# State-space outputs with tables moving and chunk columns stationary, turned by TensorE instead of through DRAM

## The reference

```python
# u: (B, S, 1024) as 64 groups of 16 channels, 64 complex states per group
bu = complex(einsum('bsgc,gpc->sbgp', ug, real(b_bar)), einsum(..., imag(b_bar)))
_, states = associative_scan(combine, (a_seq, bu), axis=0)
y = einsum('sbgp,gcp->bsgc', real(states), c_re) - einsum('sbgp,gcp->bsgc', imag(states), c_im)
y = y.reshape(B, S, 1024) + d_skip * uf
y = gelu(y)                       # then: (y @ w_glu_v) * sigmoid(y @ w_glu_g)
```

## Time and profile before

| what | value |
|---|---|
| median of 3 runs | 2946.89 us (2944.17 to 2947.73) |
| profiled execution, span of its instructions | 2941.0 us |
| TensorE busy | 2853.5 us (97%) |
| DVE, ACT, POOL busy | 968.6, 753.5, 390.1 us |
| mean granted TensorE clock | 0.988 |

### The profile page before, as it was taken

One profiled execution on the slowest core, in us unless ns is written; L12 is line 12 of the kernel. 1 busy time (PEld: TensorE's weight loads), 2 busy tenths in 40 slices (PEclk: granted clock), 3 DMA queues, 4 the chain that ended last, 5 costly groups with the idle time before them and its releaser, 6 DMA issues.

```text
span 2941.0 us, 34655 instructions
## 1 busy us (share of the span) xinstructions
PE 2853.5 (97%) x13773; PEld 2382.2 (81%) x13773; DVE 968.6 (33%) x1043; ACT 753.5 (26%) x828; POOL 390.1 (13%) x599
## 2 busy tenths in 40 slices
PE   4999999999999999999889999999999999999997
PEld 3888888888788888888678888888888888888886
DVE  4223322231232332242343232333324233333326
ACT  3222321230322222232332222222222222222223
POOL 7729007761000000000000000000000000000000
PEclk9999999998999999999999999999999999999999
DMA  5534643345333333343223323322332333232322
GB/s 133 154 123 131 123 117 94 94 95 127 92 95 97 96 97 95 99 165 99 94 72 96 97 95 97 96 97 93 100 96 96 98 94 99 93 100 93 100 93 100
DMA packets 254302, 303.44 MB, mean 103 GB/s; under 512 B 25344, under 2 KB 214848, under 8 KB 253344
## 3 DMA queue, kind: packets, MB, share of 16 engines
q1 hardware_dynamic: 235112, 265.88, 29.6%
q0 software_dynamic: 7888, 29.83, 4.0%
q10 hardware_dynamic: 11240, 6.85, 0.8%
HBM read 284.23 MB, written 18.28 MB: 103 GB/s over the span
## 4 chain that ended last, share of the span: by engine, by line
PE 95%; DVE 2%; DMA 1%; ACT 1%; issue 0%; POOL 0%; ACTq 0%; DVEq 0%
PE ps L310 21%; PE ps L311 21%; PE ps L312 21%; PE ps L347 7%; PE ps L349 7%; PE ps L348 7%; PE ps L328 2%; PE ps L332 2%; PE ps L330 2%; PE ps L580 1%; PE ps L577 1%; DMA prm<-in_ssm_log_dt 1%; PE ps L539 1%; DVE a_lo L960 1%; PE ps L555 0%; PE ps L506 0%
## 5 line engine op out<-in xcount | busy, mean ns | idle before, releaser
L298 DVE TENSOR_TENSOR w_lo<-raw,w_hi 128x1024 fp32r<-128x1024 f32 x488 | 614.1, 1258 | 1513.3 <-ACT w_hi L294 1513.3
L310 PE MATMUL ps<-a_hi,w_hi 128*128 128x512 f32 x2432 | 954.3, 392 | 3.3 <-DVE w_lo L298 1.2
L311 PE MATMUL ps<-a_lo,w_hi 128*128 128x512 f32 x2432 | 949.7, 391 | 0.0
L312 PE MATMUL ps<-a_hi,w_lo 128*128 128x512 f32 x2432 | 949.7, 391 | 0.0
L294 ACT ACTIVATE w_hi<-raw 128x1024 fp32r<-128x1024 f32 x488 | 516.7, 1059 | 1617.5 <-PE ps L312 1065.7
L310 PEld LDWEIGHTS ps<-a_hi,w_hi 128*128 128x128 f32 x2432 | 458.7, 189 | 102.7 <-DVE w_lo L298 2.8
L312 PEld LDWEIGHTS ps<-a_hi,w_lo 128*128 128x128 f32 x2432 | 458.5, 189 | 96.0
L311 PEld LDWEIGHTS ps<-a_lo,w_hi 128*128 128x128 f32 x2432 | 458.9, 189 | 94.1
L347 PE MATMUL ps<-w_hi,f_hi 128*128 128x512 f32 x704 | 273.9, 389 | 0.0
L348 PE MATMUL ps<-w_lo,f_hi 128*128 128x512 f32 x704 | 273.9, 389 | 0.0
L349 PE MATMUL ps<-w_hi,f_lo 128*128 128x512 f32 x704 | 273.9, 389 | 0.0
(11 more groups left out here) (212 smaller groups left out, 2080.6 us busy)
## 6 DMA issues: line engine op xcount, KB each, us to landing
raw<-in_w_in SPq DMA_DIRECT2D x152, 512.0 KB, 3.6
raw<-in_w_ffn_gate SPq DMA_DIRECT2D x88, 512.0 KB, 3.5
raw<-in_w_ffn_up SPq DMA_DIRECT2D x88, 512.0 KB, 3.5
raw<-in_w_ffn_down SPq DMA_DIRECT2D x88, 512.0 KB, 3.7
raw<-in_w_out SPq DMA_DIRECT2D x32, 512.0 KB, 3.7
raw<-in_w_glu_v SPq DMA_DIRECT2D x16, 512.0 KB, 3.5
raw<-in_w_glu_g SPq DMA_DIRECT2D x16, 512.0 KB, 3.5
h_d<-hc POOLq DMA_DIRECT2D x8, 576.0 KB, 3.4
```

The source lines that it names most:

```text
L298: nc.vector.tensor_tensor(w_lo[:, m % 2, :], raw[:, m % 4, :], w_hi[:, m % 2, :].bitcast(F32), ALU.subtract).then_inc(lo_ready, 1)
L310: nc.tensor.matmul(o, wh[:, k, cols], x_hi[:, kt0 + k, :], start=first and k == 0, stop=False)
L311: nc.tensor.matmul(o, wh[:, k, cols], x_lo[:, kt0 + k, :], start=False, stop=False)
L312: mm = nc.tensor.matmul(o, wl[:, k, cols], x_hi[:, kt0 + k, :], start=False, stop=last and k == 3)
```

## The change

The operands of the output matmuls change places: 64 columns of `u_all` or `s_t` are stationary and the 128 columns of a table move. The result has chunks in partitions (64 per half `gh`) and four groups x 8 positions x 16 channels in columns, so that one octet fills half of the partitions of two PSUM banks. Both halves are issued together behind a piece, `gh` innermost; `pe_chunk_inputs` gets the same order of loops. `s_t` gets a column of zeros in front, so that all 64 columns are used, and the scan takes one step less. DVE copies into `y_tok`, `pe_outputs_turned` turns it with eight transposes per pair of octets, and gelu reads PSUM. The stores to `y_d` and loads of `y_in` are gone; `h_r` has three buffers; the `B_AU` pieces use two pairs of banks instead of four.

```diff
-GELU_AT = ((), (0,), (1, 2), (3,), (4,), (5,), (6, 7), ())
+GELU_AT = ((), (), (0, 1), (2, 3), (4, 5), (6, 7), (), ())
...
-        s_t = at_kb("s_t", 160, [P, HG, 2, NCH])
+        s_t = at_kb("s_t", 160, [P, HG, 2, NCH + 1])
...
-        h_r = [at_kb(f"h_r{s}", kb, [P, OG, 2, P]) for s, kb in enumerate((185, 140, 124, 128))]
+        h_r = [at_kb(f"h_r{s}", kb, [P, OG, 2, P]) for s, kb in enumerate((185, 124, 128))]
+        y_tok = [at_kb(f"y_tok{q}", kb, [P, L, P]) for q, kb in enumerate((140, 177, 181, 120))]
...
-                if k == 5:
-                    sp.wait_ge(y_copied, OCT)
-                    store_outputs(sp, 1)
...
-            for gh in range(2):
-                for e in range(OG):
-                    for ri in range(2):
+            for e in range(OG):
+                for ri in range(2):
+                    for gh in range(2):
...
+            for e in range(OG):
+                for gh in range(2):
+                    g = group(b, gh, e)
+                    nc.tensor.matmul(out(gh, e), u_all[:, g, :], t_q[b // 2][:, g % 16, :], start=e == 0, stop=False,
+                                     skip_group_check=True)
+            for e in range(OG):
                 for ri in range(2):
-                    mm = nc.tensor.matmul(ps[:, bank, col + 1:col + NCH], h_r[b % 4][ph, e, ri, :],
-                                          s_t[ph, OG * b + e, ri, 0:NCH - 1], start=False, stop=True,
-                                          skip_group_check=True)
+                    for gh in range(2):
+                        ph = slice(NST * gh, NST * gh + NST)
+                        mm = nc.tensor.matmul(out(gh, e), s_t[ph, OG * b + e, ri, 0:NCH], h_r[b % 3][ph, e, ri, :],
+                                              start=False, stop=e == OG - 1 and ri == 1, skip_group_check=True)
+            mm.then_inc(y_made, 1)
+
+        def pe_outputs_turned(pe, q):
+
+            pe.wait_ge(y_copied, 2 * q + 2)
+            if q:
+                pe.wait_ge(gelu, 2 * q)
+            for l in range(L):
+                mm = nc.tensor.transpose(pair(3)[:, l * P:l * P + P], y_tok[q][:, l, :], ident[:, :])
+            mm.then_inc(y_turned, 1)
...
-                if k >= 4:
-                    pe.wait_ge(au_copied, k - 3)
-                piece_f(pe, B_AU + k, 0, k % 4, at_hi, at_lo, 0, True, True, lambda: pe_outputs(pe, k + 6, 0))
-                pe_outputs(pe, k + 6, 1)
+                else:
+                    pe.wait_ge(au_copied, k - 1)
+                piece_f(pe, B_AU + k, 0, k % 2, at_hi, at_lo, 0, True, True)
+                if k < 2:
+                    pe_outputs(pe, k + 6)
+                elif k < 6:
+                    pe_outputs_turned(pe, k - 2)
...
-                act.wait_ge(y_back[t % 4], 16 * (t // 4 + 1))
+                act.wait_ge(y_turned, t // 2 + 1)
...
+                if k == 6:
+                    act.wait_ge(y_turned, 4)
```

More of the change, by code:

```diff
@@ L131, in build @@
         at_lo = at_kb("at_lo", 152, [P, HEADS, SEQ], F32R)
-        s_t = at_kb("s_t", 160, [P, HG, 2, NCH])
-        sc = at_kb("sc", 176, [P, 3, 768])
-        p_t = at_kb("p_t", 185, [P, 2, 768])
+        s_t = at_kb("s_t", 160, [P, HG, 2, NCH + 1])
+        sc = at_kb("sc", 176.25, [P, 3, 768])
+        p_t = at_kb("p_t", 185.25, [P, 2, 768])
         a_raw = at_kb("a_raw", 140, [HG, 2, 2 * NST])
@@ L164, in build @@
         y_lo = at_kb("y_lo", 191.75, [P, SSM // P, SEQ], F32R)
-        y_in = at_kb("y_in", 177, [P, 4, SEQ])
         y_act = at_kb("y_act", 185, [P, 2, SEQ])
@@ L184, in build @@
         u_d = nc.dram_tensor("u_d", [L, SSM, NCH], F32, kind="Internal").ap()
-        y_d = nc.dram_tensor("y_d", [L, SSM, NCH], F32, kind="Internal").ap()
         g_d = nc.dram_tensor("g_d", [OCT, P, OG * 2 * P], F32, kind="Internal").ap()
@@ L249, in build @@
         scan_step = sem("scan_step")
-        h_in = [sem(f"h_in{s}") for s in range(4)]
+        s_zero = sem("s_zero")
+        h_in = [sem(f"h_in{s}") for s in range(3)]
         t_in = [sem(f"t_in{q}") for q in range(4)]
@@ L253, in build @@
         y_copied = sem("y_copied")
-        y_stored = [sem(f"y_stored{h}") for h in range(2)]
-        y_back = [sem(f"y_back{s}") for s in range(4)]
+        y_turned = sem("y_turned")
         gelu = sem("gelu")
@@ L363, in build @@
         out_cls = out[0].rearrange("(j c) d -> c j d", c=CLS)
[L365 to L369, removed]
         block = ctx.enter_context(nc.Block())
@@ L559, in pe_chunk_inputs, with y_bank @@
             mm.then_inc(s_made, 1)
[L561 to L573, removed]
-            for e in range(OG):
[L575 to L578, removed]
-                for ri in range(2):
-                    mm = nc.tensor.matmul(ps[:, bank, col + 1:col + NCH], h_r[b % 4][ph, e, ri, :],
-                                          s_t[ph, OG * b + e, ri, 0:NCH - 1], start=False, stop=True,
-                                          skip_group_check=True)
-            if gh == 1:
-                mm.then_inc(y_made, 1)
+        def y_bank(b, gh):
+            return 4 + (b + gh) % 2
@@ new lines, in pe_outputs, with out @@
+        def pe_outputs(pe, b):
+            if b == 0:
+                pe.wait_ge(scan_step, 3 * (NCH - 2))
+                pe.wait_ge(s_zero, 1)
+                pe.wait_ge(heads_lo, 16)
+            pe.wait_ge(h_in[b % 3], 16 * (b // 3 + 1))
+            pe.wait_ge(t_in[b // 2], 16 * L)
+            if b >= 2:
+                pe.wait_ge(y_copied, b - 1)
+            def out(gh, e):
+                return ps[NST * gh:NST * gh + NST, y_bank(b, gh), e * P:e * P + P]
+            for e in range(OG):
+                for gh in range(2):
[3 more added lines that the diff above has]
+            for e in range(OG):
+                for ri in range(2):
+                    for gh in range(2):
[3 more added lines that the diff above has]
+            mm.then_inc(y_made, 1)
@@ L627, in _ @@
             for k in range(8):
-                piece_f(pe, B_G0 + k, 0, k // 4, a_hi, a_lo, 4 * (k % 4), k % 4 == 0, k % 4 == 3,
-                        lambda: pe_outputs(pe, k - 2, 0))
-                pe_outputs(pe, k - 2, 1)
+                piece_f(pe, B_G0 + k, 0, k // 4, a_hi, a_lo, 4 * (k % 4), k % 4 == 0, k % 4 == 3)
+                if k >= 2:
+                    pe_outputs(pe, k - 2)
             for k in range(8):
@@ L633, in _ @@
                     pe.wait_ge(gated, START + k + 1)
-                if k == 2:
-                    pe.wait_ge(y_copied, OCT)
-                if k >= 4:
-                    pe.wait_ge(au_copied, k - 3)
-                piece_f(pe, B_AU + k, 0, k % 4, at_hi, at_lo, 0, True, True, lambda: pe_outputs(pe, k + 6, 0))
-                pe_outputs(pe, k + 6, 1)
+                else:
[5 more added lines that the diff above has]
+                    pe_outputs_turned(pe, k - 2)
             pe.wait_ge(au_copied, 8)
@@ L845, in act_gelu @@
             def act_gelu(t):
-                if t == 0:
-                    act.wait_ge(y_made, OCT)
-                act.wait_ge(y_back[t % 4], 16 * (t // 4 + 1))
+                act.wait_ge(y_turned, t // 2 + 1)
                 if t >= 2:
@@ L852, in act_gelu @@
                 nc.scalar.activation(y_act[:, t % 2, :].rearrange("p (c n b) -> p b c n", b=2, c=CLS),
-                                     y_in[:, t % 4, :].rearrange("p (b c n) -> p b c n", b=2, c=CLS),
+                                     pair(3).rearrange("p (b c h n) -> p h b c n", b=2, c=CLS, h=2)[:, t % 2],
                                      ACT.Gelu_apprx_tanh).then_inc(gelu, 1)
@@ L860, in _ @@
                 act.wait_ge(piece_done, B_AU + k)
-                nc.scalar.activation(mrg[:, 2 * k - 2:2 * k, :].rearrange("p a n -> p (a n)"), pair((k - 1) % 4),
+                if k == 6:
+                    act.wait_ge(y_turned, 4)
+                nc.scalar.activation(mrg[:, 2 * k - 2:2 * k, :].rearrange("p a n -> p (a n)"), pair((k - 1) % 2),
                                      ACT.Copy).then_inc(au_copied, 1)
@@ L1127, in dve_chunk_inputs @@
                 dve.wait_ge(s_made, b + 1)
-                nc.vector.tensor_copy(s_t[:, OG * b:OG * b + OG, :, :].rearrange("p e r n -> p (e r n)"),
-                                      ps[:, 6 + b % 2, :]).then_inc(s_copied, 1)
+                if b == 0:
+                    nc.vector.memset(s_t[:, :, :, 0:1], 0.0).then_inc(s_zero, 1)
+                nc.vector.tensor_copy(s_t[:, OG * b:OG * b + OG, :, 1:NCH + 1].rearrange("p e r n -> p (e r) n"),
+                                      ps[:, 6 + b % 2, :].rearrange("p (a n) -> p a n", n=NCH)).then_inc(s_copied, 1)
             dve_qkv(1, 0, lambda k: dve_chunk_inputs(k - 3) if 3 <= k < 3 + OCT else None)
@@ L1138, in dve_outputs @@
                 for gh in range(2):
-                    g = group(b, gh, 0)
-                    ins = nc.vector.tensor_copy(u_all[:, g:g + OG, :].rearrange("p e n -> p (e n)"),
```

(25 more changed lines are left out.)

## The result

The changed kernel takes 2894.22 us (median of 4 runs, 2892.4 to 2898.64), beside 2947.31 us for the one before on the same chip: a ratio of 0.9828, 95% interval 0.9816 to 0.984, 53 us less. The profiled execution's span is 2892.1 us, beside 2941.0. First the page after the change: span, busy time, clock in 40 slices.

The account below looks back on a forecast made before the run. TensorE, busy 97% of the span, bounds the kernel. The outputs' stretch (171.7 to 124.0 us) saves 47.7 and chunk inputs 6.4, so 2946.9 - 54.1 = 2892.8 us; the forecast's own range is 2886 to 2902.

Parts of the forecast that it names:

- Two at once: Output matmuls: alternating column halves overlap, 0.056 us each instead of 0.112; a block 3.04 us, eight 24.3.
- rows 7 and 8: Trace evidence for overlap: 11 matmuls touched across a half change against 7 within; 32 `L457` matmuls begun within 0.44 us.
- Chunk inputs: Chunk-input matmuls, 400 to 458 us: with `gh` innermost, 0.8 us saved in each of eight blocks, 6.4 us.
- The clock: Outputs' stretch: half-clock drops behind outputs, 41 us costing 20.6, go; rival that they stay: chance 0.17, 2911 us.
- The DRAM path is worth nothing: Outputs' stay in DRAM: no TensorE wait put down to `y_d` or `y_in`, so avoiding it is worth next to nothing.
- The wait for the table of octet 3: Block 3: TensorE waits 4.2 us for `h_r`, plus 2 us of half clock; rival without either: chance 0.12, 2887 us.
- ScalarE's chain: `B_AU` pieces: copy, two gelus and weight split hidden, except 0.9 us from a table load and 0.5 at piece 7.
- The sum: Outputs' stretch falls from 171.7 to 124.0 us, 47.7 less; with 6.4 from chunk inputs, 54.1 us less.

Follow-up runs that it names:

- the halves in turn: The changed kernel with all output matmuls of half 0 issued before those of half 1, in both phases of a block: 2899.28 us, ratio 0.9847.
- `b_joined`: The kernel before, old operands kept, with both halves of the outputs behind the piece instead of one in its middle: 2961.54 us, ratio 1.0047.
- the second trace: The changed kernel run once more, unchanged, for another trace: one run of 2891.41 us.

## Why the prediction was right

The time (2894 for 2893), the direction and the mechanism came out. By its own terms:

- *Two at once.* Right: 3.13 us a block for 3.04, and 0.89 for 0.90 of a burst of transposes. The choice between 0.112 and 0.056 was decided by rows 7 and 8, and the halves in turn confirm it: the same instructions take 5.0 us a block. This is 15 of the gain; another 21 (7.60 to 4.97 us a block) come from the operands and the ended switches between rows together. The Trainium skill's rule, "TensorE: Matmul & The Clock Gate", "Part 3: Packing small matmuls", that loads overlap only across row groups, does not hold here: the 16 `L572` instructions share all rows, and start within 652.33 to 653.36 us, 0.064 each, against 0.094 with the halves in turn (654.31 to 655.82).
- *Chunk inputs.* 6.0 us (0.75 a block) for 6.4.
- *The clock.* Right that the drops behind outputs go: 41 us at half clock, worth 20.6, became 6.8, all of it around the new wait and worth 2.2. Why was only argued (little streaming in the old block), and stays open in part: `b_joined` and the halves in turn leave two causes, the operand that moves and the switches between 128 and 64 rows.
- *The DRAM path is worth nothing.* Right for the stores.
- *The wait for the table of octet 3.* Right in place and cause, too small: 6.4 us for 4.2. The half clock behind it was right, 2.2 us for 2.0. I gave table 3 the landing time, after the first table's issue, of the last lag transfer before (44.9 us), and it was 47.9. Of that 1.0 us is a misreading: the 24.3 us of the earlier trace rows is the median of two transfers. The last one alone, issued at 654.23, took 25.0 us (the line below) and landed at 679.2, 45.9 us after the first table's issue. The other 2.0 us (1.6 in the second trace) came though as many megabytes of tables lay ahead, and I did not find out why. Weights fetched earlier on the same engines (`B_AU`'s first at 649.46, before the change at 662.83) are a candidate that was not tried alone. TensorE itself came to octet 3 0.8 us later than forecast, which shortened the wait by as much.

```profile
t_q<-k_d POOLq DMA_DIRECT2D x1, 128.0 KB, 25.0
```

- *ScalarE's chain.* Too large: 1.4 us put down for two stalls, 0.4 measured, all at piece 7, for which I had 0.5. The other, 0.9, did not come. I had set the chain of two gelus and a table load against a piece and one burst of transposes, but between the piece ahead and the next use of `w_hi` there are two bursts, so the load of 1.28 us is hidden.
- *The sum.* Predicted 54.1 us from span to span, measured 48.9: 44.6 in the stretch (47.7 predicted), 6.0 in the chunk inputs, less 0.7 by which the profiled execution had come later to these and 1.0 behind the stretch. The medians moved by 53.1, because the profiled execution of before was 6.3 under its kernel's median and that of after 2.1 under. So part of the closeness to 2893 is luck: the miss in the stretch, 3.1 us, is the honest measure. The step that was mis-sized most is the wait for the table, 2.2 of it; blocks 0.1 us longer than forecast (0.7 in all) and the stall of ScalarE that did not come (0.9 less) partly cancel.

## What to carry to other kernels

When a small product leaves half of TensorE's columns or rows free, issue matmuls that use different halves alternately: with the same shapes, the order in the instruction stream alone made the block 3.1 us or 5.0. Let the wider operand move, and put instructions that use the same rows together: the two as a pair took a block from 7.6 to 5.0 us and kept the clock at full, though no run here tells which of them does how much. And when TensorE becomes faster between fixed transfers, list which load it will reach too early, and issue loads in the order of need before buying buffers.

## What the runs showed beyond that

- Four tiles of 64x64 run at about three times the rate of single file (0.032 us against about 0.10 for an instruction with 128 columns moving), with operands in only two row halves.
- The clock can be at half with hardly any idle time: `b_joined` had 2.7 us of idle time in its stretch of 190.6 and spent about 88 us of it at half clock.
- An idle time of 6.4 us cost another 2.2 us through the clock, so that removing the wait gave 9, not 6. Only the part of the half clock in which TensorE works counts: 4.7 us of 6.8.
